# New places for the second half's dense layers among the expert steps, and gelu of the first half six steps later

## What is computed

```
h = x
xn = rmsnorm(h);  q,k,v,xc,B,C,ga,gc = split(xn @ w_in)         # 8 x 1024 columns
y_attn = stick_breaking_attention(q,k,v)                          # 16 heads of 64
y_conv = B * causal_conv3(C * xc)
h += (sig(ga) * (y_attn @ Wa) + sig(gc) * (y_conv @ Wc)) @ Wo
h += cross_attention(rmsnorm(h), rmsnorm(mem))                    # 4 heads, 256 memory tokens
xn = rmsnorm(h);  queries = xn @ w_query                          # 8 heads, product keys 128 x 128
experts, gates = top16 of top16 x top16 scores, softmax           # 128 experts per token
act = gelu(u[experts] . xn);  h += sum(gates * act * v[experts])  # tables u, v: 16384 x 1024
out = rmsnorm(h)
```

## Time and profile before

| | before |
|---|---|
| three executions | 2456.34, 2457.06, 2461.49 us (median 2457.06) |
| the profiled execution | 2465.36 us, its span 2463.5 us |
| mean granted clock of TensorE | 0.936 |
| busy share of the span | PE 90%, DVE 50%, ACT 17%, POOL 36% |
| read from HBM | 609.77 MB, 248 GB/s over the span |
| instructions | 22441 |

### The profile page before, as it was taken

How to read it: one execution, slowest core, us unless ns; L and a number is a source line. 1 busy time by engine, 2 the same in 40 slices (tenths; PEclk the granted TensorE clock), 3 DMA queues, 4 the chain that set the end, 5 groups by cost and what they waited for, 6 DMA issues and landing times.

```text
span 2463.5 us, 22441 instructions
## 1 busy us (share of the span) xinstructions
PE 2207.7 (90%) x8007; PEld 1442.7 (59%) x8007; DVE 1229.4 (50%) x3394; ACT 427.9 (17%) x947; POOL 884.7 (36%) x784
## 2 busy tenths in 40 slices
PE   8988999898897778898884398999999889999998
PEld 7567786647766666785663375444444554444443
DVE  0122100006746766775567999444444997443301
ACT  1222110111202222121111122011010321111111
POOL 0000000003632322452336655555455556556521
PEclk9999999999997888999997579999999999999999
DMA  7322344336985655898688777999999879999975
GB/s 231 102 86 71 118 154 154 103 102 223 368 285 174 197 182 183 279 380 289 207 288 293 255 237 243 349 340 337 344 335 343 284 241 331 358 358 356 362 248 170
DMA packets 252433, 613.36 MB, mean 249 GB/s; under 512 B 18676, under 2 KB 121124, under 8 KB 252324
## 3 DMA queue, kind: packets, MB, share of 16 engines
q0 software_dynamic: 110592, 402.70, 46.9%
q1 hardware_dynamic: 141120, 208.17, 24.6%
q10 hardware_dynamic: 612, 1.07, 0.1%
HBM read 609.77 MB, written 2.10 MB: 248 GB/s over the span
## 4 chain that ended last, share of the span: by engine, by line
PE 75%; DVE 19%; ACT 2%; issue 2%; POOL 1%; DMA 1%; DVEq 0%; SPq 0%; ACTq 0%; POOLq 0%
PE ps L500 28%; PE ps L704 18%; PE ps L670 14%; PE ps L512 8%; DVE u_rows L1159 5%; DVE hot_a L1210 5%; PE ps L537 3%; DVE hot_b L1206 1%; POOL u_rows L465 1%; DVE sp_lo L1013 1%; DMA wring<-in_w_in_dram 1%; DVE spb L1010 1%; PE ps L646 1%; DVE ytap L976 1%; PE ps L549 1%
## 5 line engine op out<-in xcount | busy, mean ns | idle before, releaser
L465 POOL DMA_INDIRECT u_rows<-in_peer_u_dram,idx x512 | 597.2, 1166 | 1160.2 <-DVE idx L1152 588.8
L1159 DVE CUSTOM_DVE_ANT_0 u_rows<-u_rows,xn 128x1024 f32<-128x1024 f32 x512 | 620.9, 1221 | 374.0 <-DMA u_rows<-in_peer_u_dram,idx 372.3
L500 PE MATMUL ps<-xT,wring 128*128 128x256 f32 x2560 | 595.9, 394 | 13.9 <-DVE xT L954 4.7
L500 PEld LDWEIGHTS ps<-xT,wring 128*128 128x128 f32 x2560 | 505.1, 199 | 89.5 <-issue 7.3
L670 PE MATMUL ps<-v_rows,diag 128*128 128x512 f32 x1024 | 477.8, 601 | 3.8 <-DVE hbuf L1217 3.3
L704 PE MATMUL ps<-d_rows,gates 128*128 128x512 f32 x1024 | 460.3, 592 | 0.0
L474 POOL DMA_INDIRECT v_rows<-in_peer_v_dram,idx x256 | 285.0, 1113 | 400.5 <-PE ps L670 371.2
L704 PEld LDWEIGHTS ps<-d_rows,gates 128*128 128x128 f32 x1024 | 194.6, 190 | 244.9 <-issue 244.9
L670 PEld LDWEIGHTS ps<-v_rows,diag 128*128 128x128 f32 x1024 | 192.7, 192 | 225.7 <-issue 221.5
L885 ACT ACTIVATE diag<-ident,wgt 128x128 f32<-128x128 f32 x256 | 99.6, 394 | 698.6 <-PE ps L670 599.2
L692 PEld LDWEIGHTS ps<-hot_b,hot_a 128*128 128x128 f32 x1024 | 141.4, 219 | 79.0 <-DVE hot_a L1210 71.7
(11 more groups left out here) (163 smaller groups left out, 1720.8 us busy)
## 6 DMA issues: line engine op xcount, KB each, us to landing
wring<-in_w_in_dram SPq DMA_DIRECT2D x128, 512.0 KB
d_rows<-in_peer_v_dram SPq DMA_DIRECT2D x128, 512.0 KB
wring<-in_peer_w_query_dram SPq DMA_DIRECT2D x32, 512.0 KB
wring<-in_w_branch_conv_dram SPq DMA_DIRECT2D x16, 512.0 KB
wring<-in_w_branch_attn_dram SPq DMA_DIRECT2D x16, 512.0 KB
wring<-in_w_out_dram SPq DMA_DIRECT2D x16, 512.0 KB
wring<-in_xattn_wq_dram SPq DMA_DIRECT2D x16, 512.0 KB
wring<-in_xattn_wo_dram SPq DMA_DIRECT2D x16, 512.0 KB
```

The source lines that it names most:

```text
L465: pool.indirect_dma_start(out=u_rows[:, n % URING, :], out_offset=None, in_=peer_u[0], in_offset=bass.IndirectOffsetOnAxis(ap=idx[:, g % I ...
L500: mm = pe.matmul(bank(job)[:, 0:HN], w[:, k % 4, P * b:P * (b + 1)], act[:, k, :], start=(k == 0), stop=(k == KT - 1))
L1159: dve.tensor_tensor_reduce(out=u, in0=u, in1=(xn2 if h else xn1)[:, i, :], scale=1.0, scalar=0.0, op0=ALU.mult, op1=ALU.add, accum_out=dot ...
```

## The change

The table `COST` is replaced by `PACE`, which gives the number of U steps behind each unit directly; the slots are its running sum from 26 on. The sum over `FRONT[1]` is 181, so the last unit comes at 204. The places of some units, worked out from the two tables:

| unit | before | changed |
|---|---|---|
| n1 of both tiles | 24, 24 | 26, 27 |
| q 0, k 0, v 0 | 24, 36, 48 | 28, 38, 49 |
| z of head 0 | 54 | 55 |
| y of head 15 (attention's end) | 123 | 105 |
| gc 0 | 124 | 106 |
| wo 0 | 172 | 149 |
| xo 1, n3 of both tiles | 202; 205, 206 | 177; 179, 180 |
| pq 0, pq 5, pq 8 | 207, 223, 232 | 181, 196, 204 |

Parts 5, 6 and 7 of gelu of the first half's groups move from e = 5, 6, 7 to e = 11, 12, 13. `T_SLOT` moves from 264 to 270; the first 32 chunks from steps 268 to 299 to steps 272 to 303; the first 64 blocks from 302 to 388 to 306 to 388. Nothing else moves; all operations, shapes and transfers stay.

```diff
-    T_SLOT = HSTEPS + 8
-    CH_SLOT = [HSTEPS + 12 + n if n < 32 else HSTEPS + 136 + n - 32 for n in range(CHUNKS)]
-    BLK_SLOT = [HSTEPS + 46 + n * 88 // 64 if n < 64 else HSTEPS + 170 + (n - 64) * 104 // 64 for n in range(BLOCKS)]
+    T_SLOT = HSTEPS + 14
+    CH_SLOT = [HSTEPS + 16 + n if n < 32 else HSTEPS + 136 + n - 32 for n in range(CHUNKS)]
+    BLK_SLOT = [HSTEPS + 50 + n * 84 // 64 if n < 64 else HSTEPS + 170 + (n - 64) * 104 // 64 for n in range(BLOCKS)]
...
-    COST = {"n1": 1, "q": 7, "k": 7, "v": 7, "z": 1, "c": 2, "y": 2, "cj": 3.5, "gc": 3.5, "ga": 3.5, "wc": 3.5,
-            "wa": 3.5, "wo": 7, "n2": 2, "xq": 7, "s": 3, "p": 2, "o": 1, "xo": 7, "n3": 2, "pq": 7.5}
-    S_FIRST, S_LAST = 24, 236
-    total = sum(COST.get(unit[0], 0) for unit in FRONT[1])
+    PACE = {"n1": 1.0, "q": 2.7, "k": 2.7, "v": 2.8, "z": 0.5, "c": 0.5, "y": 0.7, "cj": 1.0, "gc": 1.35, "ga": 1.35,
+            "wc": 1.35, "wa": 1.35, "wo": 2.8, "n2": 1.0, "xq": 2.7, "s": 1.5, "p": 0.5, "o": 0.3, "xo": 2.8, "n3": 1.0,
+            "pq": 2.8}
     SLOT = {}
-    seen = 0
+    reached = 26.0
     for unit in FRONT[1]:
-        SLOT[unit] = S_FIRST + int((S_LAST - S_FIRST) * seen / total)
-        seen += COST.get(unit[0], 0)
+        SLOT[unit] = int(reached)
+        reached += PACE.get(unit[0], 0)
...
+                late = 6 if g <= HG else 0
-                if 0 < g <= GROUPS and e < 8:
+                if 0 < g <= GROUPS and e < 5:
                     gelu(g - 1, e)
+                if 0 < g <= GROUPS and 5 <= e - late < 8:
+                    gelu(g - 1, e - late)
```

## The result

| | before | changed |
|---|---|---|
| executions, median | 2459.27 us (4) | 2490.10 us (4) |
| ratio, 95% interval | | 1.0119 (1.0102 to 1.0136) |
| profiled execution, its span | 2465.36, 2463.5 us | 2489.36, 2487.5 us |
| mean granted clock | 0.936 | 0.932 |

The change costs 30.8 us. Forecast were +14.6 us (2472 us) and a range up to 2486 us: the sign held, the forecast was half of what came, and the time lies outside the range.

What follows compares the result with a forecast made beforehand. Bound by dense layers in lockstep with VectorE's U steps, then VectorE's remaining U steps, then TensorE. Up to n3 -10.3 us, behind it +24.9 us: +14.6 us, median 2471.7, given as 2472 us; range 2452 to 2486 us.

Steps and rivals of the forecast that it cites:

- The start: From n1 to q of the second half: three more U steps come in front, +5.0 us.
- Attention: Second half's attention: shorter VectorE segments -11.3 us and higher clock -3.5 us, together -14.8 us.
- The waits for sp_lo: In attention's heads, TensorE's waits for VectorE's sp_lo shrink as seven U steps leave the segments, -11.3 us.
- The term of -3.5 us for the clock: In attention, shorter waits keep TensorE's clock up: -3.5 us, between 0 and -32.
- The tail: Behind n3 up to step 304: 26 more U steps, fewer stalls and slower gather issue, +27.6 us.
- the wait for wst: TensorE's idle gap in front of the tables, behind the query layer, grows from 59.7 to about 95 us.
- the chunks' -2.7: Step 304 to 392: last chunk's matmuls start later (+4.5), four fewer expert steps follow (-7.2), -2.7 us.
- the term for the weights: In q, k and v of the second half, gathers run longer beside the dense weights: +1 us (0 to +9).
- My rival on late weights: Gathers without pause delay weights: 9 us in q, k, v, 6.5 in the query layer; 2486 us, chance 0.14.
- Gates to n3: At the norm of n3, two U steps instead of three stand ahead of it: -1.5 us.
- The stall at step 203: In the query layer VectorE waits there for ScalarE's exp behind pq 5: +6.3 us.
- my two signs of being wrong: Attention shorter by over 25 us (clock above 0.93 there), or the wait for wst below 80 us.

Runs made afterwards that it cites:

- the second trace of before: The kernel before, unchanged, run again for a second trace: 2457.4 us, ratio 1.0003 to before; span of the trace 2455.3 us.
- experiment 2: The changed kernel with the old places (COST), so only later gelu and the moved tables, chunks and blocks: 2454.2 us against 2456.0 us before, ratio 0.9994.
- experiment 8: The changed kernel with VectorE waiting at second-half q, k, v units until ScalarE has taken them: 2491.1 us, ratio 1.0118 to before.
- experiment 3: The changed kernel with the first three groups' gelu at its old place, so VectorE pauses at steps 37 and 53: 2479.7 us, ratio 1.0103 to before.
- experiment 10: The kernel of experiment 7 unchanged, run again on the chip of experiment 9: 2442.9 us, ratio 0.9919 to before.
- experiment 7: Experiment 6 with n1 at step 24, first groups' gelu early, q, k, v at 3 steps a unit, pq at 3.5: 2446.8 us, ratio 0.9941 to before.
- Experiment 9: Experiment 7 with 4.1 steps for xq, 1.4 for o, 4.2 for pq: 2418.4 us against 2461.4 us before, ratio 0.9821.
- experiment 5: The changed kernel, unchanged, run again for a second trace: 2495.0 us against 2463.7 us before, ratio 1.0127.
- experiment 6: The changed kernel with 23 more U steps between attention's end and n3, where VectorE waits for TensorE: 2449.5 us against 2463.7 us before, ratio 0.9946.

## Why the forecast was half the size

**What held.** The start: 11.2 us from n1's transposes to q, 2.9 to 4.7 us more than in the traces of before, where +5.0 was forecast. Attention: -13.3 to -15.4 us for -14.8. That this met so well was in part luck. The waits for sp_lo fell by 13.6 us (14.7 against the second trace of before) and not 11.3. The term of -3.5 us for the clock isn't shown: TensorE's busy time in attention was 211.9 us, against 213.6 and 210.4 in the two traces of before, at a clock of 0.86 against 0.85 and 0.86. (The two rows are of sp_lo and sp_hi, not of one matmul; the durations do hold for both, 0.28 to 0.29 us in the one head and 0.41 in the other.) The head of the earlier trace rows changed as its order of instructions said; VectorE now:

```profile
854.58 1.01 DVE L975 SCALAR_TENSOR_TENSOR ytap<-u_pad,cols,ytap 128x256 f32<-128x256 f32 x2
855.50 1.22 DVE L1158 CUSTOM_DVE_ANT_0 u_rows<-u_rows,xn 128x1024 f32<-128x1024 f32 x1
...
857.53 1.08 DVE L1009 TENSOR_TENSOR spb<-spb,ps 128x896 f32<-128x896 f32 x1
859.62 1.09 DVE L1012 TENSOR_TENSOR sp_lo<-spb,sp_hi 128x896 fp32r<-128x896 f32 x1 [1.02 <-ACT sp_hi L818]
```

One U step between the convolution and max, none behind it, and ScalarE's copy showing for 1.02 us (forecast 1.05): the wait of 4.25 us became 2.3. The tail: n3 to step 304 was +31.2 us for +27.6; the wait for wst was met to 0.2 us. The gates stage and the blocks took no time of their own within 3 us, and the chunks' -2.7 came as -2.2 and -2.9.

**The step that failed: the term for the weights.** I put +1 us for gathers that run longer beside q, k and v, and named +9 us as its bound. It was +8.4 us by the second trace of before (+9.7 in experiment 2, where nothing else in this stretch changes). Against that trace the whole forecast is 17.6 us short (14.6 for 32.2), and this term is 7.4 us of it, the largest piece. I reasoned that "the gathers also pause here". They pause for the last 40 us before attention (the queue of the gathers moved 0.24 MB in 705:745), when TensorE no longer waited for weights; ahead of that VectorE ran from step 28 to 54 in 45 us without a stall of more than some 4 us. TensorE's waits for weights went from 2.0 to 8.3 us, and the matmuls of the stretch took 88.0 us instead of 85.9 at a clock of 0.96 instead of 0.98. In the changed kernel TensorE, in this order:

```profile
690.30 5.45 PE L499 MATMUL ps<-xT,wring 128*128 128x256 f32 x24 [1.69 <-DMA wring<-in_w_in_dram]
697.21 1.97 PE L499 MATMUL ps<-xT,wring 128*128 128x256 f32 x8 [1.46 <-DMA wring<-in_w_in_dram]
703.23 4.03 PE L499 MATMUL ps<-xT,wring 128*128 128x256 f32 x10 [4.06 <-DMA wring<-in_w_in_dram]
```

The first of the four ended at 681.3 us, 33 us behind the first q matmul, and they stop when the gathers stop. That the six slots of weights are drawn down until then is what the rates of experiment 8 say (105 GB/s against 147 needed); the slots themselves aren't in the trace. Experiment 2 (late gelu alone: +9.7), experiment 3 (stalls at 37 and 53 back: 85.6 us) and experiment 8 (the same run of steps paced: 85.7 us) tell this apart from chance and from ScalarE. My rival on late weights had the right price for this stretch (9 us), at a chance of 0.14. Its other price, 6.5 us in the query layer, wasn't met: the waits for weights there were 1.0 and 2.1 us in the two traces (4.5 us in experiment 2). And the row that I took the price from, 4.00 us in the earlier trace rows, is put down to issue there, so that it was a wait for weights isn't shown. So the stall of VectorE that gelu's move takes away was useful: it held back the gathers while TensorE needed the bytes. The direction agrees with the round by packets that the Trainium skill states ("DMA: Bandwidth & Descriptors", section "Queues, rings and completion order"): in 658:698 the weights' packets were smaller (4199 for 4.18 MB against 2979 for 10.86 MB) and got the smaller share of the bytes. Their counts weren't equal, though, and no run here varied the packets' size.

**Smaller misses, 10 us together.** Gates to n3 was +1.1 us and not -1.5: the wait at n3's norm fell by 1.4 us as forecast, but U step places moved by one in cross-attention, and TensorE waited 1.1 us more for the probabilities; the rest is in pieces below 1 us. The stall at step 203 was 9.2 us instead of 6.3, since the query layer itself was longer (67.1 against 63.0 us; the row of 1251:1318 has a clock of 0.96, and one matmul group waited 1.0 us for weights):

```profile
1300.83 0.17 DVE L1185 TENSOR_SCALAR gl<-gl 128x16 f32<-128x16 f32 x1 [9.18 <-ACT gl L876]
...
1302.78 5.45 PE L499 MATMUL ps<-xT,wring 128*128 128x256 f32 x24 [0.99 <-DMA wring<-in_peer_w_query_dram]
```

And step 392 to the last block was 1.5 to 3 us longer. Over all twelve traces this stretch varied by 6 us, and so did TensorE's busy time in it, with the clock: 541.3 and 541.4 us at 1.00 (experiments 8 and 10), 540.8 to 543.8 us at 0.99, 544.2 to 548.1 us at 0.98 (the first trace of the changed kernel, experiments 2, 7 and 9). The change didn't make this: experiments 5 and 8, with its places, had 543.8 and 541.3 us.

**The signs.** n3 was to come some 10 us earlier and came at the same time (1250.7 us against 1250.5 in the second trace of before; 1256.6 in the first, which was 4 us later from its start on): the weights and the small misses used up what attention gave. Neither of my two signs of being wrong appeared, attention shorter by over 25 us or a wait for wst below 80 us. Neither watched the weights, the term with the widest bounds upwards.

**The chances.** Slower had 0.66, rightly. The range was too narrow upwards: it ended at 2486 us because I took the weights' rival only in part, though its condition (gathers without a pause, against weights) is exactly what the late gelu makes.

**Where the gain is.** The change took steps out of attention, which was right (-9 to -16 us in every kernel that does it), and put them behind the last unit. It could have put them in front of units at which VectorE waits for TensorE anyway: experiment 6 did this alone and turned +31 us into -14 us. Experiment 9, at -43 us, has more such steps, and also the places of before in q, k and v, the first groups' gelu early and wider places for pq; what each of these gives wasn't taken apart.

## What to carry to other kernels

When a slow serial stream (here one gather and one dot per step) is interleaved with stages of another engine, count two things for each stage: the wait of the first engine there (steps put in front of it are free) and the wait of the second (steps taken out of it are gains). A step that leaves a stage needs a place in another stage's wait, or it is paid in full at the end. And before a stall of an engine that feeds transfers is taken away, look at what those transfers compete with while it lasts.

## What the runs showed of the hardware

- Two streams on the DMA, gathers of 4 KB rows on one queue and weights on another: with both together at 391 GB/s from 665 to 705 us, the stage that consumes the weights waited 8.3 us for them, all of it between 680 and 703 us. In 658:698 the gathers had 10.86 MB and the weights 4.18. With the gathers paced, the weights had 6.16 MB in the same 40 us of the stage, and it didn't wait for them (experiment 8).
- The stretch ahead of n1, which no edit touches, moved by up to 6 us on a chip and by 13 us over all traces (631.1 us in experiment 3, 644.2 us in experiment 8), and 10.6 of these 13 us are TensorE's busy time (573.3 us at a clock of 0.97, 583.9 us at 0.95). The median of before moved by 8 us between chips (2456 against 2464 us). Most stretches of the second half repeated to 1 us, the widest to 3 us. Differences of a few us between two traces need the stretch named, not the span.
- TensorE's clock was at its lower level through all of the 95 us idle run (0.51 in 1320:1410) and for the chunks that follow; the chunks didn't need the higher one: VectorE set their pace, because a chunk of 3.67 us at that level is still shorter than the 4.3 to 4.9 us in which VectorE gets to the next one-hots.
